# Stick-breaking sums of a two-block transformer kernel: fp32 matmuls replaced by single-pass matmuls on high and low halves

## The reference

```python
for i in range(S // BLOCK_Q):                 # two blocks of 128 queries
    kv_len = (i + 1) * BLOCK_Q
    z = jnp.einsum('bqhd,bkhd->bhqk', q_blk, k_blk) * scale
    mask = s_idx[None, :] < t_idx[:, None]
    log_1m = jnp.where(mask, jax.nn.log_sigmoid(-z), 0.0)
    rev = lax.cumsum(log_1m, axis=3, reverse=True)
    log_w = jax.nn.log_sigmoid(z) + (rev - log_1m)
    w = jnp.where(mask, jnp.exp(log_w), 0.0)
    outs.append(jnp.einsum('bhqk,bkhd->bqhd', w, v_blk))
```

## Time and profile before

| | us |
|---|---|
| median of 3 runs (1483.84 to 1485.80) | 1484.93 |
| the profiled execution, as timed | 1485.71 |
| its span in the trace | 1484.0 |
| PE busy in the span | 1414.4 (95%) |
| DVE busy | 915.4 (62%) |
| ACT busy | 674.8 (45%) |
| POOL busy | 14.7 (1%) |
| stick-breaking stage, first scores to last values | 427.4 to 476.3 |

### The profile page before, as it was taken

How to read it: one execution, slowest core, us unless ns; L and a number is a source line. 1 busy time by engine, 2 the same in 40 slices (tenths; PEclk the granted TensorE clock), 3 DMA queues, 4 the chain that set the end, 5 groups by cost and what they waited for, 6 DMA issues and landing times.

```text
span 1484.0 us, 23775 instructions
## 1 busy us (share of the span) xinstructions
PE 1414.4 (95%) x9772; PEld 1294.0 (87%) x9772; DVE 915.4 (62%) x1074; ACT 674.8 (45%) x769; POOL 14.7 (1%) x40
## 2 busy tenths in 40 slices
PE   6999899998999899999899999999999999999997
PEld 5989799997987799998788889999988888999996
DVE  3735655555423565555656488777766647877784
ACT  4533444444446343443344454544554345544462
POOL 0000000000002000000000000000000000000000
PEclk9989999999989999999999999999999999999998
DMA  8532354552530345554153245455535323555420
GB/s 348 174 140 86 137 175 172 199 195 99 186 114 1 114 170 195 197 175 170 64 176 109 86 142 199 170 192 185 189 121 185 110 104 114 183 188 196 170 86 29
DMA packets 31799, 224.19 MB, mean 151 GB/s; under 512 B 3552, under 2 KB 3936, under 8 KB 4720
## 3 DMA queue, kind: packets, MB, share of 16 engines
q1 hardware_dynamic: 30672, 220.21, 42.6%
q10 hardware_dynamic: 1056, 2.94, 0.6%
HBM read 222.09 MB, written 1.05 MB: 150 GB/s over the span
## 4 chain that ended last, share of the span: by engine, by line
PE 92%; DVE 4%; ACT 2%; issue 1%; DMA 1%; DVEq 0%; POOL 0%; POOLq 0%; SPq 0%; ACTq 0%
PE ring L278 19%; PE ring L235 10%; PE ring L276 10%; PE ring L236 9%; PE ring L237 9%; PE acc L235 7%; PE acc L237 7%; PE acc L236 7%; PE ring L299 2%; PE acc L411 2%; PE ring L404 1%; DVE wlo L227 1%; PE ring L503 1%; PE acc L412 1%; DMA raw<-wstream 1%
## 5 line engine op out<-in xcount | busy, mean ns | idle before, releaser
L227 DVE TENSOR_TENSOR wlo<-raw,whi 128x2048 fp32r<-128x2048 f32 x208 | 476.1, 2289 | 184.5 <-ACT whi L219 183.4
L219 ACT CAST whi<-raw 128x2048 fp32r<-128x2048 f32 x208 | 396.2, 1906 | 154.9 <-PE ring L237 86.8
L278 PE MATMUL ring<-xs,whi 128*128 128x512 f32 x1216 | 435.7, 401 | 0.0
L276 PE MATMUL ring<-xs,wlo 128*128 128x256 f32 x1216 | 344.7, 283 | 15.3 <-DVE xs L1007 9.3
L235 PE MATMUL ring<-xs,whi 128*128 128x256 f32 x960 | 279.4, 291 | 29.2 <-DVE wlo L227 16.3
L278 PEld LDWEIGHTS ring<-xs,whi 128*128 128x128 f32 x1216 | 231.3, 190 | 53.9
L236 PE MATMUL ring<-xs,whi 128*128 128x256 f32 x960 | 274.2, 286 | 0.0
L237 PE MATMUL ring<-xs,wlo 128*128 128x256 f32 x960 | 274.1, 286 | 0.0
L235 PE MATMUL acc<-hhi,whi 128*128 128x256 f32 x896 | 253.6, 283 | 1.4 <-DVE hlo L1156 1.4
L237 PE MATMUL acc<-hhi,wlo 128*128 128x256 f32 x896 | 253.5, 283 | 0.0
L236 PE MATMUL acc<-hlo,whi 128*128 128x256 f32 x896 | 253.5, 283 | 0.0
(11 more groups left out here) (203 smaller groups left out, 1326.9 us busy)
## 6 DMA issues: line engine op xcount, KB each, us to landing
raw<-wstream SPq DMA_DIRECT2D x208, 1024.0 KB, 4.9
cst<-consts ACTq DMA_DIRECT2D x1, 1025.0 KB, 14.3
hT<-xT SPq DMA_DIRECT2D x1, 1024.0 KB, 5.6
misc<-decay ACTq DMA_DIRECT2D x1, 1024.0 KB, 4.9
out<-y SPq DMA_DIRECT2D x4, 256.0 KB, 2.4
gT<-pT ACTq DMA_DIRECT2D x2, 256.0 KB, 2.6
pv<-params ACTq DMA_DIRECT2D x1, 151.0 KB
wa_sb<-wa ACTq DMA_DIRECT2D x1, 64.0 KB
```

The lines of the kernel that those rows point to most:

```text
L219: act.copy(whi[:, c % SPLIT, :], raw[:, c % RAW, :]).then_inc(hi_made, 1)
L227: dve.tensor_tensor(wlo[:, c % SPLIT, :], raw[:, c % RAW, :], whi[:, c % SPLIT, :].bitcast(f32), ALU.subtract).then_inc(lo_made, 1)
L276: pe.matmul(bank(b + t)[:, 0:256], wl[:, w], xhi[:, k, :], start=k == 0, stop=False, skip_group_check=True)
L278: mm = pe.matmul(bank(b + t), wh[:, w], xs[:, k, :, :].rearrange("p a s -> p (a s)"), start=False, stop=k == NT - 1, skip_group_check=True)
```

## The change

The log terms are split like the weights. For each head DVE, after its instruction on the log terms of head i, waits for POOL's mask of head i - 1, copies that head's 384 columns as fp32r into a slot of `hhi`, waits for that copy, and subtracts it from the log terms into the same slot of `hlo` (fp32r), which raises the new semaphore `s_hl`. There are three slots. PE waits for `s_hl` where it waited for `s_L`. It then runs, for the high half and again for the low half, one 128-column matmul with `neg` and one 384-column matmul with `tri` over both key tiles. DVE's overwriting of a log-term buffer waits for its own split rather than for the sums, and the overwriting of a slot waits for the sums of the head three before. POOL copies `tri` and `neg` once to two fp32r tiles behind the slots, as soon as the first MLP is done, and DVE waits for that once (`tri_made`).

```diff
--- before.py
+++ after.py
@@ -110,6 +110,12 @@
         rs1 = misc[:, 2048:2304]
         dec = misc[:, 0:2048].rearrange("p (h s) -> p h s", h=RET_H)
 
+        hhf, hlf = (t[:, :, :, :].rearrange("p a b s -> p (a b s)") for t in (hhi, hlo))
+        tri_r, neg_r = hhf[:, 1152:1280], hhf[:, 1280:1408]
+
+        def L_slot(h):
+            return slice((h % 3) * 384, (h % 3) * 384 + 384)
+
         def wide(ap, n):
 
             return ap.unsqueeze(1).to_broadcast([ap.shape[0], n, ap.shape[1]])
@@ -152,6 +158,7 @@
         p_hi, p_lo, sig_made = sem("p_hi"), sem("p_lo"), sem("sig_made")
         wf_made, r_col_done, r_col_copied = sem("wf_made"), sem("r_col_done"), sem("r_col_copied")
         silu_made, sq_summed = sem("silu_made"), sem("sq_summed")
+        s_hl, tri_made = sem("sb_hl"), sem("tri_made")
         z_scaled, gelu_scaled = sem("z_scaled"), sem("gelu_scaled")
         dve_own, act_own, pool_own = sem("dve_own"), sem("act_own"), sem("pool_own")
         (a1_done, a1_copied, gate_done, g_ln, g_cum, g_exp, g_kend, g_dec, g_attd, g_attc, g_attm, g_ktd, g_ktc,
@@ -498,12 +505,13 @@
                     scores(bank(h % 4), kT[head(h), h // 2, :], qT[head(h), h // 2, :]).then_inc(s_z, 1)
                 if 0 <= i - 2 < SB_H:
                     h = i - 2
-                    b, L = bank(h % 4), yf[:, (h % 2) * 384:(h % 2) * 384 + 384]
-                    pe.wait_ge(s_L, h + 1)
-                    pe.matmul(b[:, 0:256], tri, L[:, 0:256], start=False, stop=False, skip_group_check=True)
-                    pe.matmul(b[:, 128:256], neg, L[:, 256:384], start=False, stop=False, skip_group_check=True)
-                    pe.matmul(b[:, 256:384], tri, L[:, 256:384], start=False, stop=True,
-                              skip_group_check=True).then_inc(s_lw, 1)
+                    b = bank(h % 4)
+                    pe.wait_ge(s_hl, h + 1)
+                    for part in (hhf, hlf):
+                        L = part[:, L_slot(h)]
+                        pe.matmul(b[:, 128:256], neg_r, L[:, 256:384], start=False, stop=False, skip_group_check=True)
+                        mm = pe.matmul(b[:, 0:384], tri_r, L, start=False, stop=part is hlf, skip_group_check=True)
+                    mm.then_inc(s_lw, 1)
                 if 0 <= i - 4:
                     h = i - 4
                     pe.wait_ge(s_wm, h + 1)
@@ -1265,13 +1273,23 @@
 
 
             ahead(C_SB_IN, 12)
-            for h in range(SB_H):
-                s = (h % 2) * 384
-                dve.wait_ge(s_ln, h + 1)
-                if h >= 2:
-                    dve.wait_ge(s_lw, h - 1)
-                dve.scalar_tensor_tensor(yf[:, s:s + 384], bank(h % 4)[:, 0:384], 0.0, gf[:, s:s + 384], ALU.max,
-                                         ALU.add).then_inc(s_sp, 1)
+            dve.wait_ge(tri_made, 1)
+            for i in range(SB_H + 1):
+                if i < SB_H:
+                    h, s = i, (i % 2) * 384
+                    dve.wait_ge(s_ln, h + 1)
+                    if h >= 2:
+                        dve.wait_ge(s_hl, h - 1)
+                    dve.scalar_tensor_tensor(yf[:, s:s + 384], bank(h % 4)[:, 0:384], 0.0, gf[:, s:s + 384], ALU.max,
+                                             ALU.add).then_inc(s_sp, 1)
+                if i:
+                    h, s = i - 1, ((i - 1) % 2) * 384
+                    dve.wait_ge(s_L, h + 1)
+                    if h >= 3:
+                        dve.wait_ge(s_lw, h - 2)
+                    own.sync(dve.tensor_copy(hhf[:, L_slot(h)], yf[:, s:s + 384]))
+                    dve.tensor_tensor(hlf[:, L_slot(h)], yf[:, s:s + 384], hhf[:, L_slot(h)].bitcast(f32),
+                                      ALU.subtract).then_inc(s_hl, 1)
             x_low(4, lambda j: pair(acc, j))
             zero_acc(x_made, 20)
             after_product(C_SB_O, 2)
@@ -1436,6 +1454,11 @@
                 return pool.affine_select(out=d, in_=d, compare_op=ALU.is_gt, fill=0.0, base=0,
                                           pattern=[[0, 2], [1, 128]], channel_multiplier=-1)
 
+            pool.wait_ge(const_in, 16)
+            pool.wait_ge(chunk_used, C_MLP[0] + 2 * N_UP)
+            own.sync(pool.tensor_copy(tri_r, tri))
+            pool.tensor_copy(neg_r, neg).then_inc(tri_made, 1)
+
             for i in range(SB_H + 2):
                 if i < SB_H:
                     pool.wait_ge(s_sp, i + 1)
```

## The result

The changed kernel takes 1507.01 us (median; 1503.66 to 1507.16) against 1484.81: ratio 1.0144, 95% interval 1.0127 to 1.0162. It is slower by 22 us, inside the forecast range, 3 us above the point. From the first scores to the product behind the stage it is 69.9 us (424.51 to 494.41) where it was 48.8 (427.38 to 476.21), so 21 of the 22 us are lost inside the stage.

What follows compares the result with a forecast made beforehand. PE, busy 95% of the span, was taken as the bound. At half clock, late first sums and twelve steps of 4.20 us put the product 19.4 us later: 1484.93 + 19.4 = 1504, own range 1501 to 1508, overall 1488 to 1508.

Steps and rivals of the forecast that it cites:

- case A: Stick-breaking stage: clock stays at 1.2 GHz until the product behind it, 19.4 us later, 1504 us; chance 0.50.
- The idle stretch makes it fall: Stage's start: PE idle for 2.10 us before the first sums, then 1.2 GHz from 431.5 to 441.5.
- The thin sums keep it down: PE's sums shrink from 2.01 to 1.15 us at half clock; scores on 64 partitions weigh more, so 1.2 GHz stays.
- case C: Stage: clock behaves as now, back at full after 441.5; 1487 us, or 1490 with the POOL-DVE conflict; chance 0.11.
- The start: First sums of the stage: begin at 433.1 instead of 431.06, PE idling 2.0 us longer behind DVE's log terms and split.
- PE's sums: Four single-pass matmuls replace three fp32 ones: 0.80 us a head, 0.27 less, at full clock; 1.15, 0.86 less, at half.
- The ring: Wait loop through ACT, DVE and PE: two heads need 5.75 us, 2.88 a head at full clock; not binding at half.
- the saving of 0.27 turns into a loss of 0.16: Heads at full clock: waiting for DVE's split makes them 2.88 us against 2.72 now, despite shorter sums.
- The ports: POOL's mask and DVE's split exclude each other: subtraction waits 0.36 us per two heads, 2.4 us more in all.
- D: Stage: waits for DVE don't bind, PE keeps 2.45 us a head, clock as now; 1481 us; chance 0.06.
- E: PE's sums: 128-column matmuls run at fp32 price, 0.22 and 0.43 us, clock back early; 1490 or 1492 us; chance 0.04.
- B: Stage: clock comes back inside it, with some 4 to 10 heads left; 1491 to 1500 us, middle 1496; chance 0.24.

Runs made afterwards that it cites:

- the filled version with the change's order: Changed kernel, DVE's order kept, with dense matmuls added in the first steps of sums (17, 13, 2, 2): 1487.46 us, ratio 1.0011.

## Why the prediction was right

**The clock (case A).** It was the deciding step, and it held: 0.50 from 428.7 to 493.5. The grounds held in the main. "The idle stretch makes it fall" is shown by the dense matmuls in the kernel before. It is not the whole of it in the changed one: with the stretch bridged, the first thin steps lost the clock too, once with 0.65 us of idle time in 7.6. And PE's 2.0 us more of idle time, which the prediction put "right where the clock falls", were not needed: without the split the stretch is as short as before, and the clock stays down just as long. "The thin sums keep it down" is shown from both sides: without the split it stays down, with fp32 sums and the split it returns, and with dense work added to the thin sums it returns. Reading the Trainium skill's sentence (page "TensorE: Matmul & The Clock Gate") as busy time alone would have given case C; the trace has 30 us of PE busy without a gap at 1.2 GHz, so it is out.

**The start.** Forecast: first sums 433.1 - 427.4 = 5.7 us after the first scores. Measured: 430.14 - 424.51 = 5.6.

**PE's sums.** At full clock forecast 0.80, measured 0.77. At half clock forecast 1.15, measured 1.37. This is the term that was mis-sized: for full clock I took a 128-column matmul at 0.12, like one of 256, with the weight load behind it as the reason; for half clock I counted columns alone. By the same reason it is 0.21 there, twice, and the sums are 0.29 + 2 x (0.21 + 0.32) = 1.35. (The chain puts the extra on the 384-column matmul, 0.43 for 0.32 of columns, and 0.11 on the second short one; only the pair's 0.54 can be compared.) Over twelve steps this is 2.6 us. The clock's return ahead of the last values gave 0.9 of it back: from the first scores to the product I had 68.2 us, the trace has 69.9 (424.51 to 494.41). These 1.7 us are part of the way from 1504 to the 1507 of three executions. The profiled one has them too, but started the stage 2.9 us earlier; that the other three did not is likely from their times and shown by no trace. So it is partly luck that the profiled execution, 1503.66, falls right on the point.

**The ring.** Forecast 2.88 us a head at full clock without a port conflict, measured 2.85 with one, in the filled version with the change's order. Two errors cancel there: the copy is cheaper than taken, the subtraction dearer. The waits are nearly even, 0.35 and 0.39, not long and short in turn. Forecast of PE alone 2.45, measured 2.41. At half clock it doesn't bind: putting the split ahead gives 1505.4. Case C's 1487 is what the filled version with the change's order took, 1487.5. The change as made never gets there, so "the saving of 0.27 turns into a loss of 0.16" was right (2.85 against 2.72) and yet is no part of the 22 us, which are all lost at half clock.

**The ports.** POOL's mask and DVE's split do collide. The subtraction takes 0.64 us beside POOL and 0.56 without it, and POOL's mask of the weights 0.72, where a mask takes 0.41 alone, when it starts 0.19 after the subtraction. With the split ahead the copy waits for POOL in its turn, 0.54 us instead of 0.35. That agrees with the rule of the Trainium skill ("SBUF — State Buffer", "Who interferes with whom") in who blocks whom, but not in how long: POOL's second mask starts with 0.45 us of the subtraction still to come and takes only 0.31 longer. My price, 0.36 in the ring, was too high, and so was the sign I gave for it, a mask that starts only when the copy ends: the mask starts at 456.40, the copy ends at 456.60. Only the last 0.23 us of the mask lie beside the subtraction, which takes 0.08 longer.

**DVE's prices.** Subtraction 0.56 as forecast, without POOL; copy 0.35 against 0.41 taken.

**Rivals.** D (faster) needed a ring that doesn't bind and a clock as now. Neither came by itself; both had to be built, and then it gives 1478.6. E is out: the four single-pass matmuls take 1.37 us at half clock, not 1.8, and the second 128-column one 0.11 from start to start, not 0.43. B would have given 1491 to 1500; it is what the added dense work does, at the upper end (1499.6).

## What to carry to other kernels

In a stretch of many small, mixed matmuls, TensorE's clock is a resource of its own. Fewer passes on a busy TensorE can mean a thinner stream, and if the stretch begins with an idle gap, or with steps that are thinner still, it may then run at 1.2 GHz to its end: here 0.3 us saved a head at full clock became 1.7 us lost. So first look at the granted clock of the stretch and at the idle gap before its fall. Bridge the gap, and every thin step after it, with matmuls whose result nobody reads; and put a new instruction on another engine ahead of the one that waits for something else, not behind it: that was worth 0.44 us a head at full clock, and next to nothing at half clock (1505.4 against 1507.0).

## What the runs showed of the hardware that I had not expected

- Useless matmuls save time twice over: 9 of them take 3.4 us off the kernel before (1481.38), and 39 take 7 us off the changed one (1499.60).
- When the clock falls and returns differs from one execution to the next. The same GLA matmuls ran at half clock up to 107.8 in the profiled execution of the change, where the stage then began 2.9 us earlier, and beyond 110.5 in that of the kernel before; and the version with 11 dense matmuls and the split ahead took 1478.7 once and 1502 to 1504 three times.
- At 1.2 GHz the thin stream did not get the clock back in 60 us (without the split), and at 2.4 GHz full steps of it kept it for 48 us, with PE waiting 0.35 to 0.39 us in every head. Steps without the values lost it in three of four executions, in the traced one with PE idle for 0.65 of the 7.6 us ahead of the fall.
- A single-pass matmul of 128 columns costs more than its columns when other matmuls with their weight loads follow: at half clock a pair of 128 and 384 columns takes 0.54 us where the columns alone are 0.43.
